# Unread matmuls at the entry of the even attention, and w_mod pieces loaded by four transfers each

## The reference, cut to what matters

```python
def trunk_layer(l, x, cvec, prm, ctx):
    mod = jax.nn.silu(cvec) @ prm["w_mod"][l] + prm["b_mod"][l]     # 1024 x 6144 per layer
    shift1, scale1, gate1, shift2, scale2, gate2 = jnp.split(mod, N_MOD, axis=-1)
    h = rmsnorm(x, prm["norm_pre"][l, 0]) * (1.0 + scale1) + shift1
    ...
def even_mixer(h, w_in, conv_w, a_log, dt_bias, sink, out_norm, w_out, ctx):
    ...
        oa = window_ctx_attention(apply_rope(qa, cos, sin), apply_rope(ka, cos, sin), va,
                                  k_ctx, v_ctx, sink, scale)
        ob, _, _ = delta_bidir(qb, kb, vb, g, beta, s0_f, s0_b)
    ...
    out = jnp.concatenate([oa.reshape(bsz, seq, A_Q), ob.reshape(bsz, seq, B_VW)], axis=-1) @ w_out
```

## Time and profile before

| | |
|---|---|
| median of 3 runs | 1928.89 us |
| the profiled execution's own time | 1928.23 us |
| its span in the trace | 1926.4 us |
| PE busy | 1841.1 us, 96% of the span |
| DVE busy | 963.8 us (50%) |
| ACT busy | 827.9 us (43%) |
| delta rule | about 229 to 437 us |
| even attention | about 438 to 536 us |
| granted TensorE clock, mean | 0.993 of full |

### The profile page before, as it was taken

How to read it: one execution, slowest core, us unless ns; L and a number is a source line. 1 busy time by engine, 2 the same in 40 slices (tenths; PEclk the granted TensorE clock), 3 DMA queues, 4 the chain that set the end, 5 groups by cost and what they waited for, 6 DMA issues and landing times.

```text
span 1926.4 us, 36263 instructions
## 1 busy us (share of the span) xinstructions
PE 1841.1 (96%) x14824; PEld 1698.8 (88%) x14824; DVE 963.8 (50%) x1613; ACT 827.9 (43%) x1420; POOL 55.0 (3%) x76
## 2 busy tenths in 40 slices
PE   6999998888899999999999999999999999999998
PEld 3999966667799999999999887776899999999997
DVE  4433355556746655235555743344375553255555
ACT  4545422225745544124445653343464441244453
POOL 0000122220000000000000000000000000000000
PEclk9999999998999999999999999999999999999999
DMA  7222366531021223222234311110211232122243
GB/s 284 65 58 66 128 252 221 199 141 51 1 71 44 77 71 87 71 66 68 73 94 140 95 44 32 27 35 28 67 44 55 76 87 78 55 76 76 78 136 115
DMA packets 238723, 170.23 MB, mean 88 GB/s; under 512 B 20139, under 2 KB 230285, under 8 KB 232333
## 3 DMA queue, kind: packets, MB, share of 16 engines
q1 hardware_dynamic: 238604, 168.54, 28.2%
HBM read 165.08 MB, written 3.44 MB: 87 GB/s over the span
## 4 chain that ended last, share of the span: by engine, by line
PE 85%; DVE 6%; ACT 4%; issue 3%; DMA 1%; SPq 0%; ACTq 0%; DVEq 0%
PE ps L2007 46%; PE ps L2083 15%; PE ps L2040 4%; PE ps L2201 3%; PE ps L2708 2%; PE ps L2745 2%; PE ps L2704 2%; PE ps L2398 1%; PE ps L2220 1%; PE ps L2578 1%; PE ps L2451 1%; PE ps L2555 1%; PE ps L2211 1%; PE ps L2028 1%; ACT w_hi L782 1%
## 5 line engine op out<-in xcount | busy, mean ns | idle before, releaser
L782 ACT ACTIVATE w_hi<-w_raw 128x1024 fp32r<-128x1024 f32 (+4 forms) x187 | 198.6, 1062 | 559.6 <-PE ps L2007 436.0
L1366 DVE TENSOR_TENSOR w_lo<-w_raw,w_hi 128x1024 fp32r<-128x1024 f32 (+4 forms) x191 | 234.2, 1227 | 377.2 <-ACT w_hi L782 376.8
L2007 PE MATMUL ps<-h_hi,w_hi 128*128 128x322 f32 x1648 | 381.5, 313 | 3.2 <-ACT conv L972 1.7
L2007 PE MATMUL ps<-h_lo,w_hi 128*128 128x322 f32 x1648 | 380.2, 312 | 0.0
L2007 PE MATMUL ps<-h_hi,w_lo 128*128 128x322 f32 x1648 | 378.1, 310 | 0.0
L2007 PEld LDWEIGHTS ps<-h_hi,w_hi 128*128 128x128 f32 x1648 | 278.1, 189 | 4.8 <-ACT conv L1192 2.0
L2007 PEld LDWEIGHTS ps<-h_hi,w_lo 128*128 128x128 f32 x1648 | 279.1, 189 | 0.0
L2007 PEld LDWEIGHTS ps<-h_lo,w_hi 128*128 128x128 f32 x1648 | 279.1, 189 | 0.0
L2083 PE MATMUL ps<-g_hi,w_hi 128*128 128x322 f32 x352 | 110.7, 314 | 2.7 <-DVE g_lo L1850 1.6
L2083 PE MATMUL ps<-g_lo,w_hi 128*128 128x322 f32 x352 | 109.6, 311 | 0.0
L2083 PE MATMUL ps<-g_hi,w_lo 128*128 128x322 f32 x352 | 109.1, 310 | 0.0
(11 more groups left out here) (376 smaller groups left out, 3337.5 us busy)
## 6 DMA issues: line engine op xcount, KB each, us to landing
w_raw<-in_ffn_w_up SPq DMA_DIRECT2D x88, 512.0 KB, 3.7
w_mod_raw<-in_w_mod SPq DMA_DIRECT2D x40, 1024.0 KB, 6.9
w_raw<-in_ffn_w_down SPq DMA_DIRECT2D x48, 704.0 KB, 4.5
w_raw<-in_ev_w_in SPq DMA_DIRECT2D x18, 512.0 KB, 3.6
w_mod_first<-in_w_mod SPq DMA_DIRECT2D x8, 1024.0 KB, 15.6
w_raw<-in_ev_w_out SPq DMA_DIRECT2D x8, 512.0 KB, 4.3
w_raw<-in_od_w_out SPq DMA_DIRECT2D x8, 512.0 KB, 4.0
w_raw<-in_od_w_kv_up SPq DMA_DIRECT2D x24, 128.0 KB, 2.3
```

The source lines that it names most:

```text
L782: act.activation(WH[slot][:, 0:k, :], RAW[slot][:, 0:k, :], ACT.Copy).then_inc(w_hi, 1)
L1366: dve.tensor_tensor(WL[slot][:, 0:k, :], RAW[slot][:, 0:k, :], WH[slot][:, 0:k, :].bitcast(F32), ALU.subtract).then_inc(w_lo, 1)
L2007: last = pe.matmul(out, w_of(k, wi), x_of(k, xi, i), start=(k == 0 and p == 0), stop=(k == ks - 1 and p == 2))
```

## The change

Two things change on PE, one on SP. PE issues three unread matmuls into bank 7 between the last delta product and the wait for the delta's output, after a wait on the last rotated row; and four more right after the first scores. SP loads each of the 40 pieces by four transfers of 512 columns each (256 KB) in place of one of 2048 columns (1 MB), all four on the piece's semaphore, and PE's waits count 64 a piece in place of 16. What is computed is the same.

```diff
@@ -628,7 +628,9 @@
                 if u >= MSLOTS:
                     sp.wait_ge(S("mod_done"), KD + u - MSLOTS + 1)
                 l, m0 = mod_columns_of(u // KD)
-                sp.dma_start(MW[u % MSLOTS][:, :], wm[l][:, u % KD, m0:m0 + 2 * D]).then_inc(S(f"mod_landed{u % MSLOTS}"), 16)
+                for j in range(4):
+                    sp.dma_start(MW[u % MSLOTS][:, 512 * j:512 * j + 512], wm[l][:, u % KD, m0 + 512 * j:m0 + 512 * j + 512]
+                                 ).then_inc(S(f"mod_landed{u % MSLOTS}"), 16)
@@ -2306,7 +2308,7 @@ mod_first_half, and the same line in mod_piece
-                pe.wait_ge(S(f"mod_landed{u % MSLOTS}"), 16 * (u // MSLOTS + 2))
+                pe.wait_ge(S(f"mod_landed{u % MSLOTS}"), 16 + 64 * (u // MSLOTS + 1))
@@ -2525,6 +2527,8 @@
                     last.then_inc(S("os_done"), 1)
 
+            pe.wait_ge(S("a_rotated"), NT)
+            keep_busy(7, 3)
             for c in range(2):
                 pe.wait_ge(*both("o_done", c, NT))
@@ -2590,6 +2594,8 @@
                 if u < len(ALLU) and u % 2 == 0:
                     att_scores(u)
+                if u == 0:
+                    keep_busy(7, 4)
                 if 1 <= u <= len(ALLU):
                     att_turn(u - 1)
```

## The result

The changed kernel takes 1936.63 us (median of 13 runs, 1927.67 to 1940.93), the kernel before on the same chip 1929.17 (13 runs, 1926.9 to 1939.2). The ratio is 1.003, with a 95% interval of 1.0017 to 1.0042. So it is slower by 7.5 us by the medians and by 5.8 us (3.3 to 8.1) by the ratio, where 11.4 us of gain were forecast. The profiled execution took 1936.52 us, its span is 1934.7.

What follows compares the result with a forecast made beforehand. PE, busy 96% of the span, was taken to lose time at the attention's entry (holes, half clock) and to late instruction fetches in the delta rule; +0.1 - 3.8 - 8.4 + 0.7 = -11.4 us gave 1917.5, range 1914.5 to 1926.0.

Steps and rivals of the forecast that it cites:

- The entry, -3.8 and +0.1: At the attention's entry, unread matmuls fill two PE holes and keep the clock up: -3.8 us, costing +0.1 us.
- The forecast end of the stretch, 17.84 us: In the attention, first scores to those of unit 8 would take 17.84 us, as in tile 4, instead of 21.64.
- the clock stays up: Around the attention's entry, PE's granted clock would stay 1.00 (2.4 GHz) from 430 to 520 us.
- The fetch stalls, -8.4: In the delta rule, quarter-size transfers let instruction fetches come sooner, removing most of 9.4 us of PE stalls: -8.4 us.
- rival B: Delta rule stalls stay, as a fetch waits for bytes or "issue" hides something else: -3.0 us, 1925.9; chance 16%.
- The cost of the split, +0.7: In the load of w_mod, shorter rows make the first two pieces land later, 0.35 us each: +0.7 us.
- later pieces have cover: In the delta rule, later w_mod pieces cost no wait: a 41.1 us round eats eight, 29 us at 3.6 each.
- D: In the w_mod load, small transfers are served one after the other: about +140 us, 2069; chance 5%.

Runs made afterwards that it cites:

- experiment 1: The kernel before plus only the unread matmuls, pieces still in one transfer each: 1929.76 us, ratio 1.0001.
- experiment 5: The kernel before, but from the fifth piece of w_mod on only 64 of 2048 columns are loaded: 1915.78 us, ratio 0.993.
- experiment 2: The kernel before plus only the four transfers of 512 columns a piece, no unread matmuls: 1936.73 us, ratio 1.0042.
- experiment 4: The kernel before with each piece in two transfers of interleaved 512-column blocks, 2 KB packets: 1936.3 us, ratio 1.0035.
- experiment 7: The kernel before, but from the fifth piece on SP issues a piece only when the one before has landed: 1930.46 us, ratio 1.0009.
- experiment 6: The kernel before with each piece in two transfers of 1024 contiguous columns, 4 KB packets: 1935.5 us, ratio 1.0022.
- experiment 3: The kernel before with each piece in four transfers of 32 partitions and all 2048 columns, 8 KB packets: 1975.67 us, ratio 1.0244.

## Why the prediction was wrong

**The entry, -3.8 and +0.1.** The row was read correctly, and half of the mechanism works: the early fall of the clock is gone. But a single execution's dip was taken for the kernel's, so the term was too large. The forecast end of the stretch, 17.84 us, is near what full clock gives (17.44, 17.50); its start, 21.64, was 2.0 us above the mean of four profiles. The gain is 19.6 - 18.6 = 1.0 us by these profiles (0.7 with all ten that have the holes), and experiment 1 puts the change of the time between -2.3 and +2.5 us, so it is not told from none. Also wrong was that the clock stays up: it fell in three of the four profiles with the unread matmuls, later in the stretch and for 3.4 to 6.8 us.

**The fetch stalls, -8.4.** This is the step that failed: the stalls went to 12.3 us in the profile, 2.3 more than the mean of before. That "issue" is a late fetch was right, as experiment 5 shows: with hardly any load the stalls go from about 10 us to 0.2. That a fetch waits for the rest of *one transfer*, so that quarter transfers quarter the wait, is wrong.

In the trace the stalls lie 256 instructions of PE (weight loads and matmuls above all), or a multiple, apart: one block for each packet of 16 KB. From where PE enters a block to the start of the next packet, 26 to 28 of 30 waits can be matched in the delta rule of each of these profiles. The waits are 1.9 to 2.1 us on average in the four profiles of before, the longest 3.5 to 3.9 with 1 MB in a transfer (4.2 in one profile of experiment 1, whose load is the same); 2.1 to 2.3 with 256 KB, the longest 4.4 and 4.6; 1.1 with hardly any load. The size of a transfer does not shorten them.

What does set them can be read from the same traces: take the bytes that SP has issued and that no DMA engine has begun when PE enters a block. Over 184 waits of the seven profiles with 1 MB transfers (before, and experiment 1) the wait goes with them (correlation 0.86). One place at the end of a round is left out, as its wait is 3.4 to 4.1 us in all of these and in experiment 5 too.

| issued and not begun | wait, 1 MB transfers | wait, 2 KB packets (changed kernel, experiments 2 and 4) |
|---|---|---|
| under 0.5 MB | 1.2 us | 1.4 us |
| 0.5 to 1 MB | 2.0 us | 2.6 us |
| 1 to 1.5 MB | 2.7 us | 3.4 us |
| 1.5 MB and more | 3.4 us | 3.5 us |

(The two lowest cells on the right stand on seven waits each.) With as much queued, smaller transfers bring no shorter wait. From 2 MB on it does not rise further (3.3 to 3.5 us, seven waits). That was rival B's reason (a fetch waits for bytes), to which I gave 16%; and even B left out that the same bytes take longer in short packets.

A block's own matmuls cover the first 4 us or so, of which the packet and PE's start behind it take 2.3; what a wait has beyond the rest is paid in full, as in the stall above. So a longer load can make stalls longer and turn near misses into stalls. The changed kernel has 10 places; but experiments 2 and 4 have 7 and 8, like before (7 to 9), and what grew there is the single stall (mean 1.5 and 1.7 us, 1.2 to 1.4 in before).

The Trainium skill, "DMA: Bandwidth & Descriptors", section "Queues, rings and completion order", was the rule behind the term. It says that the engine drains a packet of descriptors before it turns to the next queue. As I applied it, with the transfer as the unit of the turn, the runs speak against it; whether the engine's own unit is smaller than any transfer tried, no run here shows. The Trainium skill's rule that spoke against the term, in "Runtime: NRT & Kernel Launch", section "Instruction fetch mechanics", that the crossing to the next block of 16 KiB is mostly hidden, holds in experiment 5 and not beside a full load.

**The cost of the split, +0.7.** Taken from the start alone, where PE waits 1.8 us for w_mod and not 1.0 + 0.3: +0.5, as forecast. But "later pieces have cover" looked only at when a piece lands. What a longer load does to the fetches beside it was not asked. Packets of 8, 4 and 2 KB take 309, 159 and 84 ns (medians), the load 115.0, 118.4 and 121.7 to 123.1 us of each engine's time. This sum alone does not make the loss: in experiment 7 the packets of 8 KB add up to 121.7 us too, yet with at most one piece queued it has 6.0 us of stalls and no loss.

**The clock in the delta rule** stood in no term: dips of 3.4 us or more follow some of the longer holes. Before had none, two, two and none of them there in four profiles, but the kernel of experiment 1, with the same delta rule, two, four and three: over these seven 6.8 us at half clock on average (0 to 17). The changed kernel has 10.2 us, experiment 2 20.5 and experiment 4 23.9. The mean granted clock is 0.9948 over 25 runs of before and 0.9932 over the 13 of after.

**The balance of the delta rule.** A single profile of before is again no measure: the seven profiles with 1 MB transfers take 208.4 to 214.8 us, 211.4 on average, and the changed kernel 216.9, +5.6. Stalls make 12.3 - 10.0 = +2.3 of it, waits for w_mod 1.8 - 0.8 = +1.0, and 3.4 us more at half clock can cost half of that at most. Over the runs of one kernel a line through spans and clocks rises by 0.33 us (13 runs of after) or 0.35 (25 of before) for each us at half clock, which gives 3.4 x 0.33 = +1.1. That is 4.4 of the 5.6; the rest is open. Over the three kernels with 2 KB packets (216.9, 218.6 and 222.6 us) it is +8.0: stalls +2.2, waits +0.8, and 11.4 us more at half clock, +3.8. So the clock costs there more than stalls and waits together. These shares are estimates from one profile a kernel.

**The rivals.** D (transfers served one after the other) did not happen: from issue to landing a piece of 1 MB takes 6.9 us in before, one of these 256 KB transfers 4.4, and several are under way at a time. The page's DMA issues of before and of after:

```profile
w_mod_raw<-in_w_mod SPq DMA_DIRECT2D x40, 1024.0 KB, 6.9
```

```profile
w_mod_raw<-in_w_mod SPq DMA_DIRECT2D x160, 256.0 KB, 4.4
```

The fixed 2 us for each DMA, which the Trainium skill gives in "DMA: Bandwidth & Descriptors", section "Anatomy of one DMA — SWDGE (gpsimd) path", for transfers issued from GpSimd, is not paid one by one here: 160 transfers of 4.4 us lie in a delta rule of 217 us. The Trainium skill's advice of 1 MiB transfers, from the same page, section "Measured (HBM→SBUF, 128 partitions, SWDGE, issued from GpSimd)", stands by the result; whether by the packets' size or by the transfers' number, experiments 4 and 6 don't tell. What lacked was the rival that happened: a load in short rows and more transfers makes what the fetches wait for worse, with 5% left for every slower case together.

**Left open.** Which queued bytes a fetch stands behind, and why the wait stops growing at some 3.4 us, no record tells. Nor is it shown whether the loss comes from the short rows or from the second transfer (experiment 6). Whether starting each piece just behind a fetch would keep the stalls away was not tried. Experiment 5 bounds what such a schedule could bring: 14 us. No version that loads all of w_mod was faster than the kernel before.

## What to carry to other kernels

- A dip of the clock or a stall in one profile is one draw. Before a price is put on it, look for the same stretch in other executions, or at the spread of the run times: here single runs of one kernel lie 10 us apart, as much as the whole forecast.
- Where an engine waits for "issue" beside a full DMA load, the load delays its instructions. Ask of a change to the load how many bytes it leaves *queued on the engines when a fetch comes* and how fast they drain; cutting transfers up changed neither for the better, and shorter rows drain more slowly.
- A wait with cover (pieces that land early) may still cost through what shares the DMA engines with it.

## What the runs showed of the hardware

- At full engines, packets of 8, 4 and 2 KB take 309, 159 and 84 ns: 26.5, 25.8 and 24.4 GB/s on an engine. An 8 KB packet takes 596 ns when a transfer goes to 32 partitions at a time (experiment 3).
- A late fetch costs PE more than the packet: in the changed kernel PE goes on 1.3 to 1.5 us after its end (334.38 after 332.03 + 0.92 = 332.95), in the others 1.2 to 1.6.
- A fetch of instructions waits 1.2 to 1.4 us on average with under 0.5 MB of loads queued and 3.4 to 3.5 us with 1.5 MB or more, in transfers of 1 MB as in those of 256 and 512 KB.
- A load of 40 MB beside a stage in which PE is busy nine tenths of the time costs that stage 14 us, although hardly a wait for its data is seen (1.3 us in the first profile of before).
